# Query projection between the heads of memory attention, post norms in two halves of the tokens, and the projection of p moved between the last gate products

## The reference, cut to what matters

```python
# memory attention: 4 heads of width 256, 256 memory tokens
q = (rms_norm(x, norm_cross_w) @ w_cq).reshape(1, 512, 4, 256)
logits = einsum('bqhd,bkhd->bhqk', q, k) * 256 ** -0.5
o = einsum('bhqk,bkhd->bqhd', softmax(logits), v).reshape(1, 512, 1024)
x = x + o @ w_co
# second block
x = x + rms_norm(mixed @ w_o, g_post_mix)             # norm n_post
h = rms_norm(x, g_pre_mlp)                            # norm n_mlp
f = square(relu(h @ w_up)) @ w_down
x = x + rms_norm(f, g_post_mlp)                       # norm n_pmlp
gate = sigmoid(rms_norm(x, g_ple) @ w_ple_gate)       # norm n_ple
x = x + gate * (p @ w_ple_proj)
```

## Time and profile before

| | |
|---|---|
| median of 3 runs | 2253.67 us |
| profiled execution | 2256.08 us |
| its span | 2254.3 us |
| mean granted TensorE clock | 0.988 |
| PE busy | 2173.8 us, 96% |
| PEld busy | 1770.8 us, 79% |
| DVE busy | 831.9 us, 37% |
| ACT busy | 774.4 us, 34% |
| POOL busy | 1110.8 us, 49% |

### The profile page before, as it was taken

The page is one execution under the profiler, slowest core; times in us unless marked ns, Lnnn a source line. Parts: engine busy times, 40 slices in busy tenths (PEclk is TensorE's granted clock), DMA queues, the critical chain, the costliest instruction groups (busy, mean ns, idle before and its releaser), DMA issues.

```text
span 2254.3 us, 28782 instructions
## 1 busy us (share of the span) xinstructions
PE 2173.8 (96%) x9940; PEld 1770.8 (79%) x9940; DVE 831.9 (37%) x1446; ACT 774.4 (34%) x1170; POOL 1110.8 (49%) x1476
## 2 busy tenths in 40 slices
PE   7999999999999989999999999999999979999988
PEld 5888888878886667876888888888787868888876
DVE  4222211845822546034222222207743364013136
ACT  4222223334424435323322323325543333222223
POOL 4555554753253214833555555454544546545554
PEclk9999999999999989999999999999999999999999
DMA  5332333232132112521323333322222313333331
GB/s 203 109 96 93 103 103 103 84 94 66 48 103 71 57 52 75 160 65 56 93 94 93 98 103 104 95 92 70 75 84 67 98 43 112 103 103 93 100 106 47
DMA packets 58906, 203.41 MB, mean 90 GB/s; under 512 B 6296, under 2 KB 7704, under 8 KB 58824
## 3 DMA queue, kind: packets, MB, share of 16 engines
q1 hardware_dynamic: 53568, 192.96, 27.4%
q10 hardware_dynamic: 5256, 9.30, 1.2%
HBM read 200.12 MB, written 4.74 MB: 91 GB/s over the span
## 4 chain that ended last, share of the span: by engine, by line
PE 90%; DVE 6%; issue 2%; ACT 1%; POOL 1%; DVEq 0%; ACTq 0%; POOLq 0%
PE bank L426 25%; PE bank L428 25%; PE bank L427 25%; PE bank L488 2%; PE bank L490 2%; PE bank L489 2%; PE bank L667 1%; POOL w_lo L391 1%; PE bank L690 1%; DVE gx_lo L1388 1%; DVE pn_t L1880 1%; PE bank L786 1%; PE bank L594 1%; DVE prob L1656 1%; PE bank L603 1%
## 5 line engine op out<-in xcount | busy, mean ns | idle before, releaser
L391 POOL TENSOR_TENSOR w_lo<-w_raw,w_hi 128x256 fp32r<-128x256 f32 x1456 | 1085.5, 778 | 1096.4 <-ACT w_hi L956 1095.6
L426 PE MATMUL bank<-gx_hi,w_hi 128*128 128x512 f32 x1696 | 669.8, 395 | 30.0 <-DVE gx_lo L1388 13.6
L428 PE MATMUL bank<-gx_hi,w_lo 128*128 128x512 f32 x1696 | 663.5, 391 | 0.0
L427 PE MATMUL bank<-gx_lo,w_hi 128*128 128x512 f32 x1696 | 663.1, 391 | 0.0
L956 ACT CAST w_hi<-w_raw 128x1024 fp32r<-128x1024 f32 x364 | 379.3, 1045 | 386.9 <-PE bank L428 340.6
L426 PEld LDWEIGHTS bank<-gx_hi,w_hi 128*128 128x128 f32 x1696 | 320.2, 189 | 106.0 <-issue 19.3
L428 PEld LDWEIGHTS bank<-gx_hi,w_lo 128*128 128x128 f32 x1696 | 320.2, 189 | 67.8
L427 PEld LDWEIGHTS bank<-gx_lo,w_hi 128*128 128x128 f32 x1696 | 320.6, 189 | 65.0
L426 PE MATMUL bank<-ff_hi,w_hi 128*128 128x512 f32 x352 | 136.9, 389 | 0.0
L427 PE MATMUL bank<-ff_lo,w_hi 128*128 128x512 f32 x352 | 136.9, 389 | 0.0
L428 PE MATMUL bank<-ff_hi,w_lo 128*128 128x512 f32 x352 | 136.9, 389 | 0.0
(11 more groups left out here) (325 smaller groups left out, 2699.4 us busy)
## 6 DMA issues: line engine op xcount, KB each, us to landing
w_raw<-wstream SPq DMA_DIRECT2D x364, 512.0 KB, 3.5
bias_spread<-bias_rows ACTq DMA_DIRECT2D x1, 2560.0 KB
x<-xT ACTq DMA_DIRECT2D x2, 1024.0 KB, 10.5
outT<-ple_o SPq DMA_DIRECT2D x8, 256.0 KB, 2.0
square<-bias_spread ACTq DMA_DIRECT2D x4, 256.0 KB, 2.8
rfin_row<-bias_spread ACTq DMA_DIRECT2D x4, 256.0 KB, 2.7
m_T<-memT ACTq DMA_DIRECT2D x1, 1024.0 KB, 5.3
p_T<-pT ACTq DMA_DIRECT2D x1, 512.0 KB, 4.2
```

The source lines that it names most:

```text
L391: ins = nc.gpsimd.tensor_tensor(w_lo[:, s, part], w_raw[:, s, part], w_hi[:, s, part].bitcast(F32), ALU.subtract)
L426: nc.tensor.matmul(dst, hi, rhs[0], start=first, stop=False)
L427: nc.tensor.matmul(dst, hi, rhs[1], start=False, stop=False)
L428: return nc.tensor.matmul(dst, lo, rhs[0], start=False, stop=last)
```

## The change

**Memory attention.** Only tiles 0 and 1 of cq are computed ahead of the loop. Tiles 2 to 7 stand in the loop, half a tile (12 products) ahead of each of the scores 0 to 11, and in steps 12 to 17 stand the first six chunks of `co`'s tiles 0 and 1. Scores use two banks instead of three, values banks 7 and 4.

**Post norms.** The last four tiles of o2 and the last two of down_b are computed first for tokens 0 to 255, then for tokens 256 to 511 (`split_tail`); norms, post steps and squares work on halves, so that the first half's norm and post steps stand beside the second half's products. `pn` is written to PSUM and the norm row is read from there. The next stage's first three tiles are also computed by halves (`group_by_halves`), in banks 2 to 4, and the fourth in bank 5. GpSimd adds squares only after it has split all four units of the ring.

**Projection of p.** Its four units stand between the last five tiles of the gate: gate 3, project 0, row, project 1, gates 4 and 5, project 2, gates 6 and 7, project 3. VectorE multiplies from PSUM, and the eight copies are gone. Weights are streamed in this order, and `split_unit` takes two quarters instead of four for p's units, whose second half is empty.

```diff
+            def split_tail(stage, rhs, chunks, hooks):
+                start, count, per = SPLIT[stage]          # o2: (4, 4, 1), down_b: (6, 2, 2)
...
+                for a in range(2):
+                    for j in range(count):
...
+                        for k in range(chunks):
...
+                            mm = products(U % RING, k % UC, bank[n % 2][:, 0:HT], [r[:, tok(a)] for r in rhs(k)],
+                                          k == 0, k == chunks - 1)
...
+            def group_by_halves(stage, name, hooks):
...
+                for a in range(2):
+                    for k in range(DC):
+                        pe.wait_ge(sem("gx_lo_done"), gx_count(name, a * DC + k + 1))
+                        late = a == 0 and k < 3
+                        for j in range(2 if late else 3):
+                            part(a, k, j)
+                        if late and k == 2:
+                            for kk in range(3):
+                                part(a, kk, 2)
...
+            def beside_heads(n):
+                if n < 12:
+                    one_tile("cq", 2 + n // 2, range(n % 2 * 4, n % 2 * 4 + 4), gx)
+                elif n < 16:
+                    one_tile("co", n % 2, range((n - 12) // 2 * 2, (n - 12) // 2 * 2 + 2), ox, ready=ox_ready)
+                elif n < 18:
+                    one_tile("co", n % 2, range(4, 6), ox, ready=ox_ready)
...
             for n in range(XH * TT + 4):
+                beside_heads(n)
                 if n < XH * TT:
                     x_score(n)
...
-            tiles("o2", gx, DC, 4, peel=1, ready=gx_ready("branch2"))
-            boundary("n_post", "o2")
-            tiles("up_a", gx, DC, 4, peel=1, ready=gx_ready("post"),
-                  hooks=norm_hooks("n_mlp", "post", together=3), banks=4, together=3)
+            tiles("o2", gx, DC, 4, peel=1, ready=gx_ready("branch2"), count=4)
+            split_tail("o2", gx, DC, {(1, 0, 7): stat0, (1, 1, 3): row0})
+            group_by_halves("up_a", "post", {(0, 3): stat1, (0, 5): row1})
+            tail_of_group("up_a", {1: stat, 7: row})
...
+            split_tail("down_b", up, HC, {(1, 0, 7): stat0, (1, 0, 11): row0})
+            group_by_halves("ple2a", "pmlp", {(0, 3): stat1, (0, 5): row1})
...
+            gate(3, {1: stat})
+            project(0)
+            row()
+            project(1)
+            gate(4)
+            gate(5)
+            project(2)
+            gate(6)
+            gate(7)
+            project(3)
...
             # ScalarE, after o2 (a is the half of the tokens)
+            half_root("n_post", 0)
+            ahead("o2", 0, 4, 5)
+            half_square("o2", "o2", y_o2, 1, 0)
+            post("post", "g_pre_mlp_2", range(0, 2))
+            ahead("o2", 0, 4, 6)
+            half_square("o2", "o2", y_o2, 1, 1)
+            ahead("o2", 0, 4, 7)
+            post("post", "g_pre_mlp_2", range(2, 4))
+            half_square("o2", "o2", y_o2, 1, 2)
+            half_square("o2", "o2", y_o2, 1, 3)
+            ahead("up_a", 0, 4, 0)
+            post("post", "g_pre_mlp_2", range(4, 6))
+            half_root("n_post", 1)
+            post("post", "g_pre_mlp_2", range(6, 16))
...
             # VectorE, one post step: idx 0..7 are the tiles of the first half, 8..15 of the second
+                    row, pn = bank[7 - a][:, 0:HT], bank[7 - a][:, HT:S]
+                    link(nc.vector.scalar_tensor_tensor(out=pn, in0=src[:, m, tok(a)], scalar=col(weight, m), in1=row,
+                                                        op0=ALU.mult, op1=ALU.mult))
+                    nc.vector.tensor_tensor(x[:, m, tok(a)], pn, x[:, m, tok(a)], ALU.add)\
...
+            half_column("n_post", 0)
+            o2_half(1, 0)
+            o2_post(0, 1)
+            o2_half(1, 1)
+            o2_post(2, 3)
+            o2_half(1, 2)
+            o2_half(1, 3)
+            o2_post(4, 5)
+            half_column("n_post", 1)
+            o2_post(*range(6, 16))
```

More of the change, by code:

```diff
@@ L108, in norm_count @@
             n = NORMS.index(name)
+            if step == "ready":
+                n -= sum(m[:-1] in ("n_post", "n_pmlp") for m in NORMS[:n])
             more = {"root": 2, "row": 1}.get(step, 0)
@@ new lines, in _, with gate @@
+            (_, stat), (_, row) = norm_hooks("n_ple", "pmlp")
+            pe.wait_ge(sem("p_lo"), 2)
+            def gate(m, hooks=()):
+                U = PLE_UNIT[m]
+                pe.wait_ge(unit_lo, U + 1)
+                if m in (4, 5, 6):
+                    pe.wait_ge(tile_free, TILE0["ple2a"] + m - 2)
+                if m == 7:
+                    pe.wait_ge(sem("proj_out"), 1)
+                for k in range(DC):
+                    mm = products(U % RING, k, bank[PLE_BANK[m]][:, :], gx(k), k == 0, k == DC - 1)
+                    if k in dict(hooks):
+                        dict(hooks)[k]()
+                mm.then_inc(unit_done, 1)
@@ new lines, in _ @@
+            ahead("down_b", 0, 8, 12)
+            half_square("down_b", "down", f_acc, 0, 0)
+            half_square("down_b", "down", f_acc, 0, 1)
+            half_root("n_pmlp", 0)
+            ahead("down_b", 0, 8, 13)
+            post("pmlp", "g_ple_2", range(0, 2))
+            ahead("down_b", 0, 8, 14)
+            half_square("down_b", "down", f_acc, 1, 0)
+            ahead("down_b", 0, 8, 15)
+            post("pmlp", "g_ple_2", range(2, 4))
+            half_square("down_b", "down", f_acc, 1, 1)
@@ new lines, in _ @@
+            for m in range(6):
+                dve.wait_ge(unit_done, UNIT0["down_b"] + m * 2 + 2)
+                nc.vector.tensor_tensor(f_acc[:, m, :], bank[m % 2][:, :], f_acc[:, m, :], ALU.add).then_inc(tile_free, 1)
+                add_square("down", m)
+            down_half(0, 0)
+            down_half(0, 1)
+            half_column("n_pmlp", 0)
+            down_post(0, 1)
+            down_half(1, 0)
+            down_post(2, 3)
+            down_half(1, 1)
+            down_post(4, 5)
@@ L2010 @@
     upw = _units(v["w_up_2"][0])
+    ple = _units(v["w_ple_gate_2"][0])
     stream = np.concatenate([
```

452 lines of the change are left out of this document (304 added, 148 removed).

## The result

The changed kernel takes 2234.74 us, the median of four runs (2233.81 to 2237.89); the kernel before, run beside it, 2254.36 (2253.28 to 2255.93). The ratio is 0.9912, 95% interval 0.9900 to 0.9923: 19.6 us faster, where 17.5 were forecast. 2236.2 us was predicted, and the range (2225 to 2250) held the time. The profiled execution is the slowest of the four: 2237.89 us, with a span of 2236.1 us and a mean granted clock of 0.992.

What follows compares the result with a forecast made beforehand. TensorE was taken to bound the kernel, with gains only where it stood idle or slow. Memory attention 3.1, n_post 6.8 and n_pmlp with projection 7.6 us summed to 17.5, from 2253.67 to 2236.2 us; range 2225 to 2250.

Steps and rivals of the forecast that it cites:

- third term: n_pmlp, the projection of p and the tail: end at 2246.7 instead of 2254.3, a gain of 7.6 us.
- the entry into weight products: Memory attention's loop: 18 switches from float32 to weight products at 0.2 us, 3.6 us of its 11.2 us of waits.
- The wait ahead of the last values: Memory attention's last head: nothing stands in steps 18 and 19, so a wait of 2.2 us stays.
- The half product: Last tiles of o2 and down_b: a product of 256 columns takes 0.119 us, gaps included.
- The rival of unhidden weight loads: Tails and groups: weight loads don't hide behind 256-column products, 0.227 us each, 2285 us in all; chance 0.03.
- The post step: VectorE's half step in the post norms: 1.26 us bare plus 0.24 charged for GpSimd, 1.5 in all.
- The schedule of n_post: From o2's tail through up_a's first tiles: group ends at 1832.7 against 1841.35, 8.6 us earlier, 6.8 net.
- T: The end of the first-half tiles, from which the schedule counts; for o2 forecast at 1796.1, for down_b at 2166.6.
- The wait at the seventh tile: up_a after n_post: the next norm's row comes later, so the seventh unit is late, 1.8 us of new wait.
- Better overlap: Post steps at the bare 1.26 us, entries at 0.11, co's waits hidden: 2227 us; chance 0.15.
- VectorE contended: Every post step takes 2.4 us because GpSimd always runs or PSUM is slow to write: 2251 us; chance 0.12.
- Low clock: TensorE at 1.2 GHz for ten us in each of the two post-norm groups: 2244 us; chance 0.13.

Runs made afterwards that it cites:

- run 1: The kernel before with only the memory attention of the kernel after: 2246.00 us, ratio 0.9961.
- run 2: The kernel after with memory attention put back as before; halved post norms and moved projection stay: 2243.95 us, ratio 0.9948.
- run 4: The kernel before with only pn and the norm row of the post steps written and read in PSUM, no halves: 2243.85 us, ratio 0.9951.
- run 3: The kernel after with pn and the norm row of the post steps put back in SBUF, halves and order kept: 2250.34 us, ratio 0.9977.
- run 11: The kernel after with n_mlp's row behind chunk 4, co's first products spread, and ScalarE's first-half squares ahead of weight casts: 2227.87 us, ratio 0.9880.
- run 5: The kernel after with n_mlp's row behind chunk 4 instead of chunk 7 of up_a's fourth tile: 2234.08 us, ratio 0.9910.
- run 6: The kernel after with co's first products spread over steps 16 to 18 and behind the loop: 2230.43 us, ratio 0.9888.

## Why the prediction was right

**The sum.** 17.5 us were forecast and 19.6 measured, and the mechanisms that the prediction named are in the traces. That the sum came so close is luck in part, since two terms miss by about as much in opposite directions: memory attention gave 4.3 us more than its term, `n_post` 3.5 less in the profiled execution. Only the third term (7.0 against 7.6) came out by itself.

**Memory attention: mechanism right, size too small.** 3.1 us were taken, 7.4 measured (M, runs 1 and 2). The mis-sized term is the entry into weight products: 0.2 us each, 3.6 in all. Its first step is 0.09 longer, but the float32 work ahead of it is 0.08 shorter (1026.70 and 1026.84 above), so it costs almost nothing. The wait ahead of the last values was 1.4, not 2.2, and each of the new ones 0.9, not 1.0. That makes 3.2 and about half a microsecond of small things left of the 11.2 us, so 7.4 or a little more gained. The spell of low clock of the loop before was among the 11.2, and it is gone with the waits: the three profiles with the old loop (before, runs 2 and 4) have it at 1012, the ten with the new loop don't.

**The half product: right.** 0.12 us apart against 0.119. The rival of unhidden weight loads is refuted: with it 2285 us would have been measured. (Its threshold of 0.155 us a half product doesn't come out of its own terms: 17.5 us over 384 half products are 0.046 each, so 0.165.) The rule on overlap of the Trainium skill (TensorE: Matmul & The Clock Gate, What overlaps and what doesn't), taken by itself, doesn't hold for these products.

**The post step: right, 1.41 against 1.5.** So was the reason, only `gx_lo` of the three being stretched; run 3 shows what steps cost without PSUM operands.

**The schedule of n_post: mechanism right, 1.5 us late, and more given back.** The factor of part 2 was at T + 24.4 (T = 1788.2, first pn of it 1812.63) against T + 23.0, and the group ended at T + 38.1 (1826.3) against T + 36.6. ScalarE's casts ahead of squares (run 11: 0.65 us) and the low clock at 1806 (0.8 between the stats, of which 0.4 is left at the end of the group) account for most of it. The wait at the seventh tile was 2.6 against 1.8, and its reason was right (run 5). 6.8 were forecast; the profiled execution gave 3.3 (18.2 of span less 7.4, 7.0 and the 0.5 ahead of the marks), with 2.0 of low clock in it (0.4 and 1.6, see above). Without that it is 5.3, and the term was 1.5 too large. The mean of four executions is 2.6 us below the profiled one.

**n_pmlp, projection, tail: right.** 7.0 against 7.6; group at T + 36.3 against 35.5; 40.1 behind it to the last product's start against 40.5 to the end of products; 4.3 against 4.1 behind the last product.

**What it missed altogether.** The prediction gave the second block's gain to laying the norm beside products, and took PSUM operands as a safeguard (0.24 instead of some more per step). Run 4 shows that the operands alone bring 11.9 us, run 3 that the halves without them bring nothing or less: its B is 3.4 us longer than before. A sum worked out from step lengths holds both, and didn't price them apart.

**The other rivals.** Better overlap (2227) didn't come: co's waits weren't hidden, though entries were even cheaper than it said. Run 6 is that case for memory attention and gave 3.5 us. VectorE contended (2251) has the time that run 3 measured, 2250.34, and contention is its cause there; but the rival laid it on the second half's steps at 2.4 us each, and these take 1.26 to 1.81 in run 3, while the first half's take up to 2.7. So its time is met in part by luck, and its condition is SBUF operands. Low clock came in spells of 3 us, not ten: one on the first half products of up_a, none in the rest of the groups.

## What to carry to other kernels

Where VectorE sets the pace and GpSimd works beside it, first move an operand of each of VectorE's instructions with two SBUF inputs into a free PSUM bank: two lines did most of what a rewrite in halves with them did, and a step at full width takes less than two at half width (2.30 against 2.82 us). When a change holds several ideas, price each alone in the prediction; a right sum says nothing on which of them earns it. Float32 products that wait on a chain through other engines can be interleaved with weight products at next to no cost an entry, if something is left for the last steps as well. And before two profiles are compared to a microsecond, look where the clock was low in each: it moved stretches of the same code by up to 1.7 us here.

## What the runs showed of the hardware

- VectorE writes a PSUM bank at SBUF's price: undisturbed, pn takes 0.48 us at 128 x 256 and 0.74 at 128 x 512, in either memory.
- An instruction of VectorE with two SBUF inputs beside GpSimd took up to 2.5 times as long (0.48 to 0.8 or 0.96 at 256 columns, the kernel after and run 3; 0.74 to 1.24 or 1.84 at 512, run 4); pn and x with a PSUM input kept theirs in every row of the post steps.
- A reduced-precision product with a new 128 x 128 weight tile takes 0.12 us at 256 columns and 0.23 at 512, hundreds in a row.
- The first weight product behind float32 work has a step of 0.31 to 0.63 us instead of 0.23, and the float32 group ahead of it ends 0.08 to 0.4 us sooner than ahead of other float32 work, so that the change-over costs next to nothing.
- The low clock comes in spells of about 3.4 us, alone or a few in a row. One cost 1.6 us where TensorE set the pace and 0.4 where VectorE did, and profiles of the same code differ by them, which is why single profiles couldn't settle differences under 2 us.
